# 93 weight units: one 512-column pass of the weights' high half over both halves of the activations

## The reference

```python
def squared_relu_mlp(x, w_up, w_down):
    return jnp.square(jax.nn.relu(x @ w_up)) @ w_down

for i in range(DEPTH):          # DEPTH = 2; dsa_mixer for i = 0, gla_mixer for i = 1
    mix = ...
    h = layer_norm(DN_ALPHA * h + mix, ln_mix_g[i], ln_mix_b[i])
    h = layer_norm(DN_ALPHA * h + squared_relu_mlp(h, mlp_w_up[i], mlp_w_down[i]), ln_mlp_g[i], ln_mlp_b[i])
```

## Time and profile before

| | us |
|---|---|
| median of 3 runs | 1397.33 (1395.53 to 1398.47) |
| the profiled execution | 1394.16 |
| its span | 1392.3 |
| PE busy | 1326.4 (95%) |
| PE weight load busy | 1272.3 (91%) |
| DVE busy | 928.1 (67%) |
| ACT busy | 627.4 (45%) |

### The profile page before, as it was taken

One profiled execution on the slowest core, in us unless ns is written; L12 is line 12 of the kernel. 1 busy time (PEld: TensorE's weight loads), 2 busy tenths in 40 slices (PEclk: granted clock), 3 DMA queues, 4 the chain that ended last, 5 costly groups with the idle time before them and its releaser, 6 DMA issues.

```text
span 1392.3 us, 25125 instructions
## 1 busy us (share of the span) xinstructions
PE 1326.4 (95%) x10604; PEld 1272.3 (91%) x10604; DVE 928.1 (67%) x1448; ACT 627.4 (45%) x805; POOL 0.2 (0%) x4
## 2 busy tenths in 40 slices
PE   6889999999998899999999999999899999999897
PEld 6866999999998799999999999889898989999797
DVE  6783576466647767646665458888876665999943
ACT  5334454354444244534435444454445455555431
POOL 0000000000000000000000000000000000000000
PEclk9975999999999899999999999999999999999999
DMA  8320325545334133554532543334445241444430
GB/s 330 115 91 0 122 104 198 184 178 191 115 122 152 61 121 105 198 184 179 195 138 94 209 159 120 118 127 150 141 172 203 92 152 61 152 181 157 175 121 31
DMA packets 28361, 198.41 MB, mean 142 GB/s; under 512 B 3296, under 2 KB 3808, under 8 KB 4592
## 3 DMA queue, kind: packets, MB, share of 16 engines
q1 hardware_dynamic: 27072, 194.00, 38.7%
q10 hardware_dynamic: 1200, 3.14, 0.6%
HBM read 196.08 MB, written 1.05 MB: 142 GB/s over the span
## 4 chain that ended last, share of the span: by engine, by line
PE 69%; DVE 23%; ACT 3%; issue 3%; DMA 1%; DVEq 0%; ACTq 0%
PE lin L422 19%; PE lin L424 18%; PE lin L423 18%; DVE wlo L1307 7%; DVE conv L1748 3%; PE lin L504 2%; PE att L589 2%; PE att L497 2%; DVE fconv L1922 1%; PE att L556 1%; ACT whi L906 1%; PE att L573 1%; DVE fconv L1921 1%; DVE fconv L1923 1%; PE lin L527 1%
## 5 line engine op out<-in xcount | busy, mean ns | idle before, releaser
L422 PE MATMUL lin<-xh,whi 128*128 128x256 f32 x1936 | 556.2, 287 | 17.2 <-DVE xl L1317 11.8
L1307 DVE TENSOR_TENSOR wlo<-raw,whi 128x2048 fp32r<-128x2048 f32 x183 | 418.7, 2291 | 215.2 <-ACT whi L906 214.0
L423 PE MATMUL lin<-xl,whi 128*128 128x256 f32 x1936 | 550.8, 284 | 0.0
L424 PE MATMUL lin<-xh,wlo 128*128 128x256 f32 x1936 | 550.5, 284 | 0.0
L906 ACT ACTIVATE whi<-raw 128x2048 fp32r<-128x2048 f32 x183 | 348.5, 1906 | 179.5 <-PE lin L424 172.7
L422 PEld LDWEIGHTS lin<-xh,whi 128*128 128x128 f32 x1936 | 375.0, 194 | 21.4 <-DVE wlo L1307 10.6
L423 PEld LDWEIGHTS lin<-xl,whi 128*128 128x128 f32 x1936 | 375.0, 194 | 0.1
L424 PEld LDWEIGHTS lin<-xh,wlo 128*128 128x128 f32 x1936 | 374.5, 193 | 0.0
L422 PE MATMUL lin<-fh,whi 128*128 128x256 f32 x512 | 143.4, 280 | 0.0
L423 PE MATMUL lin<-fl,whi 128*128 128x256 f32 x512 | 142.8, 279 | 0.0
L424 PE MATMUL lin<-fh,wlo 128*128 128x256 f32 x512 | 142.8, 279 | 0.0
(11 more groups left out here) (309 smaller groups left out, 1645.5 us busy)
## 6 DMA issues: line engine op xcount, KB each, us to landing
raw<-units_dram SPq DMA_DIRECT2D x183, 1024.0 KB, 4.8
h<-x_dram SPq DMA_DIRECT2D x1, 1024.0 KB, 6.8
memT<-mem_dram ACTq DMA_DIRECT2D x1, 1024.0 KB, 4.8
out_dram<-h SPq DMA_DIRECT2D x4, 256.0 KB, 2.0
consts<-consts_dram ACTq DMA_DIRECT2D x1, 867.5 KB, 12.2
narrow_a<-narrow_a_dram ACTq DMA_DIRECT2D x1, 544.0 KB, 14.1
vec<-vectors_dram ACTq DMA_DIRECT2D x1, 245.5 KB, 16.9
posi<-pos_dram ACTq DMA_DIRECT2D x1, 128.0 KB, 8.0
```

The source lines that it names most:

```text
L422: mm(out, w[0], a[0], start=first, stop=False)
L423: mm(out, w[0], a[1], start=False, stop=False)
L424: return mm(out, w[1], a[0], start=False, stop=last)
L1307: v.tensor_tensor(wlo[u % RING][:], raw[u % RING][:], whi[u % RING][:].bitcast(f32), ALU.subtract).then_inc(lo_ready, 1)
```

## The change

In 93 units (`ao` 4, the MLPs' up and down units 64, `gk` 2, `go` 4, `aq`, `ak`, `fq`, `fk` 2 each, `fd` 11) the two halves of the activation lie side by side in one tile (`xhl`, `fhl`, `ghl`), and a weight tile makes two passes in place of three: its high half over all 512 columns into a whole bank, and its low half over the 256 columns of the activation's high half. The two halves of the bank are added when it is read out. An up unit now fills two banks, one for each output block, where it filled one. The eviction changes with it:
- up units of the MLPs: ScalarE copies the first half of each bank (two copies of 256 columns in place of one relu of 512), VectorE adds the second half of each, and the square takes in the relu as a max with 0
- down units and `fd`: VectorE reads the first half as before, then adds the second
- `ao`, `go`: for each output block one multiply-add, one add and the running sum
- `gk`, `aq`, `ak`, `fq`, `fk`: ScalarE's first-half copies, VectorE's adds

All other units keep three passes. The diff, cut to its core:

```diff
-    units("ao", 4); norm("ln0", True)
+    units("ao", 4, 2); norm("ln0", True)
-            units(f"up{layer}{half}", 8); units(f"dn{layer}{half}", 8)
+            units(f"up{layer}{half}", 8, 2); units(f"dn{layer}{half}", 8)
...
-        xh = sbuf("xh", [P, DB, S], f32r)
-        xl = sbuf("xl", [P, DB, S], f32r)
+        xhl = sbuf("xhl", [P, DB, 2, S], f32r)
+        xh, xl = xhl[:, :, 0, :], xhl[:, :, 1, :]
...
+            def paired_pass(o, w, a, first, last):
+                if last:
+                    mm(o[:, 0, :], w[1], a[:, 0, :], start=False, stop=False)
+                    return mm(o[:], w[0], a, start=False, stop=True)
+                mm(o[:], w[0], a, start=first, stop=False)
+                return mm(o[:, 0, :], w[1], a[:, 0, :], start=False, stop=False)
...
+            def pair_up(u, j, g=None):
+                arrived(u, g)
+                for m in range(2):
+                    o = bank(j + m, g, 8)
+                    for k in range(DB):
+                        last = paired_pass(o, tile(u, m * DB + k), xhl[:, k, :, :], k == 0, k == DB - 1)
+                    last.then_inc(job_done, 1)
...
                 for k in range(UT):
                     if first is not None and k % 2 == 0:
                         pe.wait_ge(flo, first + k // 2 + 1)
-                    last = three(o[:, 0, :], tile(u, k), (fh[:, k, :], fl[:, k, :]), k == 0, k == UT - 1)
+                    last = paired_pass(o, tile(u, k), fhl[:, k, :, :], k == 0, k == UT - 1)
...
 # ScalarE, up unit
-                            j = JOB[up, i]
-                            high_part(U0[up] + i + AHEAD, g, j)
-                            filled(act, j, g)
-                            f(relu[i % 2][:], lin[j % RING][:], ACT.Relu).then_inc(evac[j % RING], 1)
+                            high_part(U0[up] + i + AHEAD, g, JOB[up, i], 8)
+                            for m in range(2):
+                                j = JOB[up, i] + m
+                                filled(act, j, g, 8)
+                                f(relu[i % 2][:, m, :], lin[j % RING][:, 0, :], ACT.Copy).then_inc(half_out, 1)
...
 # VectorE, up unit
                             low_part(U0[up] + i + AHEAD, g)
-                            evacuated(dve, JOB[up, i], g)
-                            v.tensor_tensor(sqr[i % 2][:], relu[i % 2][:], relu[i % 2][:], ALU.mult).then_inc(sqr_done, 1)
+                            for m in range(2):
+                                j = JOB[up, i] + m
+                                dve.wait_ge(half_out, per(HALVES[up] + 2 * i + m + 1, g, 8))
+                                d = relu[i % 2][:, m, :]
+                                read_out(v.tensor_tensor(d, d, lin[j % RING][:, 1, :], ALU.add), j)
+                                evacuated(dve, j, g, 8)
+                            v.scalar_tensor_tensor(out=sqr[i % 2][:], in0=relu[i % 2][:], scalar=0.0, in1=relu[i % 2][:], op0=ALU.max, op1=ALU.mult).then_inc(sqr_done, 1)
...
 # VectorE, down unit
-                                ins = v.tensor_tensor(z[:, m, :], z[:, m, :], p[:, 0:1, :], ALU.add)
-                            read_out(ins, j)
+                                link(v.tensor_tensor(z[:, m, :], z[:, m, :], p[:, 0:1, :], ALU.add))
+                            read_out(v.tensor_tensor(z[:, m, :], z[:, m, :], p[:, 1:2, :], ALU.add), j)
```

More of the change, by code:

```diff
@@ L451, in unit_first, with pair_first @@
                 last.then_inc(job_done, 1)
+            def pair_up(u, j, g=None):
[5 more added lines that the diff above has]
+                    last.then_inc(job_done, 1)
+            def pair_first(u, j, event, g=None):
+                arrived(u, g)
+                o = [bank(j + m, g, 8) for m in range(2)]
+                for c in range(4):
+                    have(event, c + 1)
+                    for m in range(2):
+                        for k in (2 * c, 2 * c + 1):
+                            last = paired_pass(o[m], tile(u, m * DB + k), xhl[:, k, :, :], k == 0, k == DB - 1)
+                        if c == 3:
+                            last.then_inc(job_done, 1)
             def unit_down(u, j, first, g=None):
@@ L488, in ups, with pair_ups @@
                         unit_up(U0[name] + i, JOB[name, i])
+            def pair_ups(name, event=None):
+                for i in range(COUNT[name]):
+                    if event and i == 0:
+                        pair_first(U0[name], JOB[name, 0], event)
+                    else:
+                        pair_up(U0[name] + i, JOB[name, i])
             def have(event, n=4):
@@ L871, in _, with fu_up @@
             norm("pre_ffn")
+            def fu_up(i, g):
+                arrived(U0["fu"] + i, g)
+                o = bank(JOB["fu", i], g)
+                for m in range(2):
+                    for k in range(DB):
+                        last = three(o[:, m, :], tile(U0["fu"] + i, m * DB + k), (xh[:, k, :], xl[:, k, :]), k == 0, k == DB - 1)
+                last.then_inc(job_done, 1)
             unit_first(U0["fu"], JOB["fu", 0], "ffn")
@@ L1055, in _ @@
                 copy("gq", i, two(gqT, i), 128 ** -0.5)
-            for i in range(2):
-                copy("gk", i, two(gkT, i))
+            first_halves("gk", gkT)
             j = JOB["alow", 0]
@@ L1120, in _ @@
             split("mix", z, is_scaled("pre_mix"))
-            for i in range(2):
-                copy("aq", i, two(aqT, i))
+            first_halves("aq", aqT)
             evacuated(act, JOB["fg", 0])
@@ L1576, in _ @@
             next_low("gq")
-            next_low("gk")
+            for i in range(2):
+                next_low("gk", i)
+                second_half("gk", i, gkT)
             for i in range(2):
@@ L1648, in _ @@
                 evacuated(dve, JOB["gq", i])
-                evacuated(dve, JOB["gk", i])
+                for m in range(2):
+                    evacuated(dve, JOB["gk", i] + m)
             for l in range(6):
@@ L1725, in _ @@
             link(v.memset(scpad[:, :, 0:2], 0.0))
-            next_low("aq")
+            for i in range(2):
+                next_low("aq", i)
+                second_half("aq", i, aqT)
             j = JOB["fg", 0]
```

130 lines of the change are left out of this document (78 added, 52 removed).

## The result

The changed kernel has a median of 1424.09 us (1422.12 to 1424.53), the kernel before, run beside it on the same chip, 1396.43 us. The ratio is 1.02, with a 95% interval of 1.0188 to 1.0212: slower by 2%, in the direction forecast and outside the range (1395 to 1416). It is the time that rival (e) gave.

The account below looks back on a forecast made before the run. TensorE was taken as the bound, with the VectorE-ScalarE loop of up units only 0.26 us per unit behind. -9.2 + 8.2 + 8.8 = +7.8 us on the 1397.33 us median gave 1405.1 us, range 1395 to 1416.

Parts of the forecast that it names:

- rival (e): In the changed units, 512 columns cost twice 256, so loads weren't the price: 1424 us; chance 0.06.
- Part 1: A weight tile in the 93 units: 334 ns with fh/fl, 336 with xh/xl, a gain of 19 or 24 ns.
- the upper bound, cost by columns: Price of a weight tile in the 93 units: 353 and 360 ns, no gain.
- Part 2: Stages where only TensorE counts (ao, go, gk, aq, ak, fq, fk, fd): -9.2 us.
- Part 3: The MLPs: longer eviction makes the loop 6.40 us and TensorE waits; +4.1 us a layer, +8.2 us for two.
- Part 4: The four first down units: half clock after TensorE's idle time, 2.2 us each, 8.8 us in all.
- (a): MLPs: the loop never reaches TensorE; faster, 1367 us, chance 0.06; a weaker form, 1393.5 us, chance 0.06.
- (b): Changed units: tiles at 325 ns, with the clock loss; 1396.5 us; chance 0.10.
- (c): First down units: no half clock after the gaps; -1.0 us, 1396.3 us; chance 0.08.
- (d): Changed units: an extra charge per pass stays, tiles at 344 and 348 ns; 1415 us; chance 0.14.

Follow-up runs that it names:

- the reordered kernel: The changed kernel with VectorE's low part moved behind the square in the up units: 1391.96 us, ratio 0.9962; run once more, 1392.77 us, ratio 0.9967.

## Why the prediction was wrong in size and right in kind

**What bounds the kernel.** Right. The loop was the second limit, 0.26 us behind TensorE, and became the first.

**Part 1, the price of a tile: the step that failed.** The term is "216 + 118 = 334 ns with fh/fl, 216 + 120 = 336 ns with xh/xl". Measured 351 and 352; the wide pass takes 232 and 235 ns, not 216. The reasoning took the 11 to 13 ns above 106.7 for a load that outlasts its stream. The rows it was nearest to the earlier trace rows are fp32 passes, another type: their 216 ns don't carry over to fp32r. A row that spoke against it was there: passes of 256 columns cost 118 with fh and 120 with xh, where a load that sticks out would be as long beside both. I had said that no row explains the difference, and the upper bound, cost by columns, was written down and given 0.06. The passes of 256, 384 and 512 columns show that bound to hold within some 2%.

**Part 2.** -9.2 forecast. Measured in the same stages: -1.9 (ao, gk, go), -1.0 (aq to fk), -1.0 (fd), together -3.9 us. A consequence of part 1 (down units, too, start 5.62 us apart and not 5.34), and a little better than rival (e)'s +0.45, since a few ns per tile are left. That the adds hide in these stages held.

**Part 3.** The mechanism held in every link: the adds lengthen the loop fully, a unit waits for the bank of the unit two before it, the first down unit starts late (229.6 for 228.4) and stands at its 15th tile (4.5 us forecast, 4.5 measured, four times). The loop is 6.50 us for 6.40: from the first add's start to the square it is 0.99 us (209.63 to 210.62), where I had 0.90; the second add starts 0.54 us after the first, the square 0.45 after the second. With 7 loops in each of four halves that is 2.8 us. With no gain in the tile the section's own sum was +17.4; 17.4 + 2.8 is 20.2, and with the clock's share taken out 20.0 us were measured. The step mis-sized is again part 1's.

**Part 4.** Half clock after each of the four waits: right. 2.2 us each was forecast, 1.35 to 1.6 measured, 6.0 for 8.8. One such stretch at 239.4 lasts 3.4 us, of which half is lost, 1.7.

**What the sum left out.** Unchanged stages lost 6.2 us: 7.7 in gate0, gate1 and out, less 1.5 in s. TensorE did the same passes there at a lower clock. gate1 and out, before, then after:

```profile
979.00:1014.00 35.00, 29.48 (x225) 28.59 (x225) 26.94 (x37) 15.36 (x19) 0.00 (x0) 0.95 0.41 142
...
1059.00:1089.00 30.00, 27.10 (x224) 26.52 (x223) 17.71 (x23) 14.42 (x16) 0.00 (x0) 1.00 0.51 181
```

```profile
1005.00:1042.00 37.00, 31.46 (x218) 30.66 (x218) 26.27 (x36) 15.28 (x18) 0.00 (x0) 0.86 0.40 145
...
1087.00:1119.00 32.00, 28.56 (x224) 27.98 (x223) 17.64 (x22) 14.28 (x16) 0.00 (x0) 0.95 0.50 169
```

These stages have short idle times before and after the change alike; which of them is followed by half clock differs between kernels, and between two executions of one kernel. Set against the kernel before as in the table, the reordered kernel, traced twice, has 0, 0, +2.8 and +2.1 us in s, gate0, gate1 and out the first time, and -1.5, +3.0, +1.4 and +2.7 the second; the kernel with down units undone has nothing in any. The kernel before with one line of the MLPs moved, in which the change is absent, has -1.5, +2.9, +1.3 and -0.1. So 2.6 of the 6.2 us came without the change too, and one kernel differs from itself by 0.7: how much of the rest belongs to the change isn't shown. Why one idle time is followed by half clock and a like one isn't, no run here settles.

The same goes for the kernel's start, which ends 1.1 us later in the changed kernel before any unit that the change touches has run. The stretch from 31.0 to 34.6 us in the kernel before, in the changed kernel, and in the kernel before with the one line moved:

```profile
31.00:34.60 3.60, 3.60 (x20) 2.59 (x20) 3.40 (x5) 1.62 (x1) 0.00 (x0) 1.00 0.90 325
```

```profile
31.00:34.60 3.60, 3.60 (x8) 1.54 (x7) 3.57 (x5) 1.89 (x2) 0.00 (x0) 0.53 0.84 296
```

```profile
31.00:34.60 3.60, 3.60 (x7) 1.73 (x6) 3.53 (x6) 1.69 (x1) 0.00 (x0) 0.56 0.94 312
```

The changed kernel ran there at half clock, and so did the third, whose start is that of the kernel before; it too is 1.0 us later at the end of this part. The kernel with down units undone starts as the changed one does, had full clock there and is 0.4 us later. The 1.1 us are thus, but for 0.4 at most, a matter of the execution that was traced, not of the change.

**The rivals.** (e) named the right mechanism, and its number, 1424, came true partly by luck, since errors cancel in it. Above its terms came the loop (2.6 us), the unchanged stages (6.2) and the start (1.1); below them the clock in the MLPs (6.0 for 8.8) and part 2 (-3.9 for +0.45). (a) and (b) fell with the 351 ns; (c) fell with the clock of 0.50 behind each wait; (d), 344 and 348 ns by a charge on each pass over a stream of 0.417 ns a column, was nearer than the forecast, but from 256 to 512 columns each column adds (232 - 118) / 256 = 0.445 ns. Chance 0.06 for (e) was too low: of three readings of the same 118 ns, none of them shown by an fp32r row of another width, it deserved a third, and the range would then have reached 1424. The direction was right for the reasons given. Of the 20 us between the 7.8 forecast and the 27.7 measured, the price of a tile makes 14.5 (5.3 in part 2, 17.4 - 8.2 = 9.2 in part 3).

## What to carry to other kernels

Before cutting the work of the engine that bounds a stage, add up the loop that runs across the other engines for one unit: once it is as long as the bound, an added eviction step counts in full, and the cut counts for nothing. If the loop holds a long operation that the next engine doesn't need, move it behind the one that it does need; here one moved line turned 2% slower into 0.3 to 0.4% faster. And measure the price of a pass in its own type at two widths before counting on hidden weight loads.

## What the runs showed of the hardware

- fp32r passes with a weight load each: medians of 118 to 120, 176 and 227 to 235 ns for 256, 384 and 512 columns at the high clock, and 0.83 ns a column at the low one. The excess of 6 to 12% over 0.417 ns a column was seen at the high clock alone.
- A whole bank written by one pass costs no more than its two halves written by two: 351 ns a tile against 353.
- An idle time of 4.5 us of TensorE was followed by half clock four times of four, at 1.35 to 1.6 us each; with small passes in that time the clock stayed at 1.00. Shorter idle times were followed by it in one execution and not in another of the same kernel.
- VectorE's 256-column adds, with 0.42 us of work each and a wait for their own semaphore, are followed after 0.54 and 0.45 us in the loop; without such a wait the next operation starts some 0.08 us before the end of the one in front (211.06 + 0.69 against 211.67).
